# One core of Trainium2: block 1's first query, turned copy and scores moved behind the first query chunk, and new places for the first gathers

## The chip, the core and the metric

The kernel runs on one core of a Trainium2 chip. The metric is the device time of one launch in microseconds (us). The data are 32-bit floats throughout.

## The reference, cut to what matters

Two transformer-like blocks work one behind the other on 256 tokens of width 1024. The change lies in the last part of the second block: the end of the cross attention and the feed-forward stage with looked-up experts (PEER). For every token and each of 8 heads that stage picks 16 of 16384 experts by two small top-16 searches, and adds their outputs:

```python
def block(xb):                                   # 128 tokens, called for two blocks
    qh = (xb @ w_pq).reshape(T, P_HEADS, 2, P_KEY_DIM)
    s1 = einsum('thd,nd->thn', qh[:, :, 0], sub_keys1)
    s2 = einsum('thd,nd->thn', qh[:, :, 1], sub_keys2)
    v1, i1 = top_k(s1, 16);  v2, i2 = top_k(s2, 16)
    cand_s = v1[..., :, None] + v2[..., None, :]
    top_s, pos = top_k(cand_s.reshape(T, 8, 256), 16)
    eidx = the 16 expert numbers of pos
    g = softmax(top_s)
    a = gelu(einsum('thkd,td->thk', expert_down[eidx], xb))
    return einsum('thk,thkd->td', g * a, expert_up[eidx])
h = h + peer_ffn(rmsnorm_2(h, g_ffn), ...)
return rmsnorm_2(h, g_final)
```

## The kernel before, in words

**Layout.** One program per engine, tied by semaphores that only count up. Each engine takes its instructions in the order in which they are written down, so a wait holds up all that stands behind it on that engine.

**Groups, rows, steps.** The PEER stage has 16 groups g = 0 to 15: g // 8 is the block of 128 tokens (t), g % 8 the head (h). A group has 16 rows; row i of group g is called row g.i here. A row is one indirect DMA, which fetches for each of the 128 tokens one expert's down and up vector, 8 KB, so 1.05 MB in all (`gathers_pool`, L2058; the DMA is L2079). For each group the vector engine works in four steps q of four rows (`STEPS0` for group 0, `STEPS` for the others). A step is: the four dot products with the token (`down_dve`, L2083), a part of the search for a later group (`route_dve`), then, after ScalarE's gelu of the four results (`gelu`, L1954), the coefficients (`coef_dve`) and the weighted sums of the up vectors (`up_dve`, L2123). From group 1 on, some rows are "turned": ScalarE makes a diagonal matrix of the coefficients and TensorE adds the row (`weigh`, L1872). The indices of group 1 are searched for whole behind step 1 of group 0. Step 0's gelu of group 1, like those of steps 0 to 3 of group 0, stands among ScalarE's query work, at places written out by hand.

**Places.** A row is fetched into one of 16 places of 2048 floats per partition (`GPAIR`, L1125). Many of them are memory that earlier work still uses. `SOON` names those that are free early; group 0 uses only these, in turn, so its later rows wait until an earlier row's sum is made. `late` gives the memory of the others, `LATEWAIT` (L2054) what the Pool queue waits for before it uses one for the first time: the end of a query chunk (`s_chunk`), which frees a ring buffer, or the scores of a head (`s_ps`). Place 13 is ring buffer 2 and waits for the end of the last query chunk, before and after the change.

**Queries.** Head 0 has a query of its own, made per token block from the weights PQ0 (`query0_pe`, L1611), so that group 0 can start early: block 0's while block 1's projection is still to come. Heads 1 to 7 take one weight chunk each, called c1 to c7 here (`queries(h)`, L1866): 16 matmuls over all 256 tokens. TensorE writes a chunk into two of the four banks of psD, and ScalarE evicts it (`pair_act`, L1158). Three matmuls into chunk c(h), TensorE makes the scores of head h - 1 (`scores`, L1857), for which c(h-1) must have been evicted; ScalarE scales those (`scored`, L1907). The weights of c1 to c4 and c7 lie in the ring (c7's are loaded by the SP queue when c3 has ended, L2252), those of c5 and c6 in PQ5 and PQ6, fetched by the Pool queue. `xturn_pe` (L1626) turns block 1's state back to tokens along partitions, `xturn_act` scales it into XTOK, the other operand of the dot products.

**Order around the change.** TensorE (`blocks_pe`, L1635): block 0's projection and turn, query, scores and turned copy; block 1's cross output, residual and projection; the turn of block 1's state; block 1's query for head 0 (L1667, L1668), its turned copy (L1669) and its scores (L1670, L1671); then c1 to c7. ScalarE has the matching evictions at the end of `blocks_act` (L1800 to L1804), then in `peer_act` eight diagonals and, for each h, what L1918 to L1931 say. The Pool queue loads PQ5 (L2333), for which it waits until block 1's residual is in, and goes on to the gathers. Rows 0.4 to 0.8 wait each until the row four before it has landed (L2075).

Of the kernel before, what the change touches and what calls it, by code (L numbers as in the profile page):

```python
# [59 lines left out]
SLOT = {i: k for k, i in enumerate(i for _, turned in STEPS for i in turned)}  # L60
NT = len(SLOT)
SLOT.update({12: SLOT[5], 14: SLOT[6]})
SOON = [4, 5, 6, 9, 10, 11, 12, 0, 3]

MQK_SCALE = MQK ** -0.5
MAGIC = 1.5 * 2.0 ** 23
# [98 lines left out]
def build(nc, a):  # L165
# [875 lines left out]
    def ff2_act(dst, T):  # L1041
        for mg in range(4):
# [77 lines left out]

    slot = lambda v: v.rearrange("p k t -> p (k t)")[:, 0:2 * D]
    soon = [carve([2 * D]) for _ in range(6)] + [VT[:, 0:2].rearrange("p a d -> p (a d)"), slot(ZS), slot(SQ)]
    late = {1: slot(feat[:, 3]), 2: slot(ring[:, 3]), 7: slot(ring[:, 0]), 8: slot(ring[:, 1]), 13: slot(ring[:, 2]),
            14: slot(XN), 15: slot(feat[:, 4])}
    GPAIR = [soon[SOON.index(i)] if i in SOON else late[i] for i in range(PTOP)]  # L1125
    XP = soon[3].rearrange("p (n h s) -> p n h s", n=4, h=2)
# [409 lines left out]
    XTURN = {(0, 0): psD[:, 2], (1, 0): psD[:, 3], (0, 1): psD[:, 2], (1, 1): psD[:, 3]}  # L1536
    XSUM = {(0, 0): psD[:, 0], (0, 1): psD[:, 1], (1, 0): psD[:, 2], (1, 1): psD[:, 3]}
    HTURN = {(0, 0): psD[:, 2], (0, 1): psB[:, 0], (1, 0): psD[:, 0], (1, 1): psD[:, 1]}
    QBANK = {(0, 0): psB[:, 1], (0, 1): psD[:, 0], (1, 0): psB[:, 0], (1, 1): psB[:, 1]}
    SBANK = {(0, 0): psD[:, 1], (0, 1): psD[:, 2], (1, 0): psD[:, 2], (1, 1): psD[:, 3]}  # L1540
    s_xw = sem("s_xw")
    s_acc, s_ht, s_xh, s_rs, s_h3 = (sem(n) for n in ("s_acc", "s_ht", "s_xh", "s_rs", "s_h3"))

# [67 lines left out]
    def query0_pe(t, m):  # L1611
        if t:
            nc.tensor.wait_ge(s_ttc, m + 1)
        for k in range(KT):
            if m == 0 and k % 4 == 0:
                nc.tensor.wait_ge(s_xh, 2 * t + k // 4 + 1)
            mm = nc.tensor.matmul(QBANK[t, m][:, 0:P], PQ0[:, k, m * P:(m + 1) * P], XN2[:, k, blk(t)], start=(k == 0),
                                  stop=(k == KT - 1))
        mm.then_inc(s_qh, 1)

    def score0_pe(t, x):
        nc.tensor.wait_ge(s_qe, 2 * t + x + 1)
        (nc.tensor.matmul(SBANK[t, x][:, 0:PK], QH[:, x, blk(t)] if t else QH0[:, x], SKT[:, x], start=True, stop=True)
         .then_inc(s_ps, 1))
# [10 lines left out]
    def blocks_pe():  # L1635
        for j in range(4):
            chunk_pe(FIRST["xq"], j, XN2, T2, fresh=5 if j == 0 else None)
            if j:
                cross_scores_pe(j - 1)
        cross_scores_pe(3)  # L1640
        cross_turn_pe(0, 0)
        cross_turn_pe(1, 0)
        residual_pe(0)
        cross_out_pe(0, 0)
        cross_turn_pe(0, 1)
        project_pe(0, (0, 1), range(4))
# [12 lines left out]
        xturn_pe(0)
        cross_out_pe(1, 0)  # L1660
        cross_out_pe(1, 1)
        residual_pe(1)
        project_pe(1, (0, 1), range(8))
        project_pe(1, (2, 3), range(8))
        hturn_pe(1, 0)
        hturn_pe(1, 1)
        query0_pe(1, 0)  # L1667
        query0_pe(1, 1)  # L1668
        xturn_pe(1)  # L1669
        score0_pe(1, 0)  # L1670
        score0_pe(1, 1)  # L1671

    XSCALE = float(XD) ** -0.5

# [75 lines left out]
        nc.scalar.activation(dst, QBANK[t, m][:, 0:P], ACT.Identity).then_inc(s_qe, 1)  # L1750

    def score0_act(t, x):
        nc.scalar.wait_ge(s_ps, 2 * t + x + 1)
        if x == 0:
            nc.scalar.wait_ge(s_rs, t + 1)
        dst = SCO[:, t, x] if t else SCO0[:, x]
        (nc.scalar.activation(dst, SBANK[t, x][:, 0:PK], ACT.Identity, scale=F7[:, t, 2:3])
         .then_inc(s_psc, 1))
# [9 lines left out]
    def blocks_act(first_gate, first_gelu):  # L1768
# [28 lines left out]
            ins.then_inc(s_xh, 1)  # L1797
        state_root_act(1)
        first_gelu()
        for m in range(2):  # L1800
            query0_act(1, m)
        xturn_act(1)
        for x in range(2):
            score0_act(1, x)  # L1804

    (s_sk, s_ps, s_psc, s_tt, s_ttc, s_eid, s_io, s_gel, s_coef, s_usev, s_uset, s_diag, s_fin, s_fsq, s_frt) = (
        sem(n) for n in (
# [42 lines left out]
    def peer_pe():  # L1850
# [4 lines left out]
        HOME.update({FIRST["pq"] + 4: (PQ5, s_mem, 32), FIRST["pq"] + 5: (PQ6, s_sk, 64)})  # L1855

        def scores(h):  # L1857
            nc.tensor.wait_ge(s_psc, max(h + 2, 4))
            nc.tensor.wait_ge(s_dev, FIRST["xq"] + 4 + h)
            for t in range(2):  # L1860
                for x in range(2):
                    mm = nc.tensor.matmul(psB[:, h % 2, (2 * t + x) * PK:(2 * t + x + 1) * PK],
                                          QH[:, 2 * h + x, t * P:(t + 1) * P], SKT[:, x], start=True, stop=True)
            mm.then_inc(s_ps, 1)

        def queries(h):  # L1866
            if h == 2:
                nc.tensor.wait_ge(s_psc, 4)
            chunk_pe(FIRST["pq"], h - 1, XN2, T2, clear=FIRST["xq"] + 2 + h,
                     mid=(lambda: scores(h - 1)) if h > 1 else None, place=3)  # L1870

        def weigh(t, g, fixed=1, first=False):  # L1872

# [31 lines left out]

    def peer_act(link):
        def scored(h):  # L1907
            nc.scalar.wait_ge(s_ps, h + 4)
            for t in range(2):
                ins = nc.scalar.activation(SCO[:, t, 2 * h:2 * h + 2],  # L1910
                                           psB[:, h % 2, t * T2:(t + 1) * T2].rearrange("p (x n) -> p x n", x=2),
                                           ACT.Identity, scale=F7[:, t, 2:3])
            ins.then_inc(s_psc, 2 if h == PH - 1 else 1)
# [2 lines left out]
            ins = nc.scalar.activation(DIAG[:, k], ident[:, :], ACT.Identity, scale=col("g_final_2", k))  # L1916
        ins.then_inc(s_io, 1)
        for h in range(1, PH):  # L1918
            if h == 6:
                coefficients(0, 3)  # L1920
            if h > 1:
                scored(h - 1)
            if h == 4:
                coefficients(0, 2)
            if h == 6:
                gate(1)
            if h == 7:
                gelu(1, 0)
            pair_act(FIRST["pq"], h - 1, QH[:, 2 * h:2 * h + 2])
            if h == 1:  # L1930
                coefficients(0, 1)  # L1931
        scored(PH - 1)
        nc.scalar.wait_ge(s_xs, 6)
        for g in range(1, 2 * PH):
# [79 lines left out]
    def route_dve(g, part, link, t=0, first=False):  # L2014
# [5 lines left out]
        if part == 0:  # L2020
            for r in ((0, 1), (1, 2)) if first else ((0, 2),):
                r = slice(*r)
                if t == 0:
                    nc.vector.wait_ge(s_psc, r.stop if first else g + 4)
                if not first:
                    link(nc.vector.tensor_scalar(SCOH, SCO.rearrange("p t x n -> p (t x) n")[:, bass.ds(2 * g, 2)], 1.0,
                                                 None, ALU.mult))
# [12 lines left out]
        if part == 3:  # L2040
            oh = OH.rearrange("p c k j -> p (c k) j")
            wide = [P, 2 * PTOP, PTOP]
            if first:
# [7 lines left out]
                                            in1=SELK[:, 1], op0=ALU.mult, op1=ALU.add).then_inc(s_eid, 1))  # L2051


    LATEWAIT = {1: (s_ps, 7), 2: (s_chunk, FIRST["pq"] + 4), 7: (s_chunk, FIRST["pq"] + 1),  # L2054
                8: (s_chunk, FIRST["pq"] + 2), 13: (s_chunk, FIRST["pq"] + 7), 14: (s_ps, PH + 3), 15: (s_ps, PH + 3)}


    def gathers_pool():  # L2058

        last = {}  # L2060
        for g in range(2 * PH):
            nc.gpsimd.wait_ge(s_eid, g + 1)
            for i in range(PTOP):
                b = pair(g, i)
                if b in last:
                    nc.gpsimd.wait_ge(*used(*last[b]))
                elif b == 3:
                    nc.gpsimd.wait_ge(s_qh, 4)
                elif g == 0 and i in (6, 7):
                    nc.gpsimd.wait_ge(s_h3, 4)  # L2070
                elif g == 0 and i == 0:
                    nc.gpsimd.wait_ge(s_xo, 4)
                elif b in LATEWAIT:
                    nc.gpsimd.wait_ge(*LATEWAIT[b])
                if g == 0 and 4 <= i < len(SOON):  # L2075
# [58 lines left out]
    def peer_dve(link, looped):  # L2134
# [47 lines left out]
        for g in range(2 * PH):  # L2182
# [4 lines left out]
            for q in range(len(steps(g))):  # L2187
                if g % PH == 0 and q == 0:
                    dve.wait_ge(s_ttc, 2 * (g // PH) + 2)
                down_dve(g, q, g)  # L2190
                if g == q == 0:
                    rstd_dve(1)
                for h, part in routes(g, q):
                    route_dve(h, part, link, h // PH)
# [62 lines left out]
    def _(pool):  # L2257
# [71 lines left out]
        g.iota(IOI, pattern=[[1, PTOP]], base=0, channel_multiplier=0).then_inc(s_io, 1)  # L2329
        pool.wait_ge(s_io, 1)  # L2330
        g.tensor_copy(IOTA, IOI).then_inc(s_io, 1)
        pool.wait_ge(s_xs, 5)
        pool.dma_start(PQ5.rearrange("p k n -> p (k n)"), a["pq5"]).then_inc(s_mem, 16)  # L2333
        gathers_pool()

    @block.scalar
# [268 lines left out]
```

## Time and profile before

| | us |
|---|---|
| median of three timed runs | 1513.57 (1513.55 to 1515.67) |
| the profiled execution's own time | 1514.97 |
| its span, first to last instruction | 1513.2 |

| engine | busy, share of the span |
|---|---|
| PE (TensorE matmul) | 84% |
| DVE (vector engine) | 64% |
| POOL | 34% |
| ACT (ScalarE) | 23% |

The profiled execution is 1.4 us above the median, and its span leaves out 1.8 us around the first and the last instruction. Times of rows are counted from the span's start. The mean granted clock of TensorE over the span is 0.912 of its full speed. The PEER stage begins near 841 us with block 0's first query; its first gather is issued at 855 us. From about 870 us to 1500 us the row of the page that gives the DMA engines' share in 40 slices stands at 9 tenths or more in every slice.

How to read it: a timeline row gives start, duration, engine, line, operation and operands, and in brackets the idle time of the engine just before it with what ended it. A DMA's row on POOL is only its issue. The DMA view gives for a stretch each kind of transfer issued in it, with its median time from issue to landing. Matmuls are pipelined and their ends are modelled.

### The profile page before, as it was taken

How to read it: one execution, taken by the hardware profiler on the slowest of the kernel's cores; microseconds unless marked ns; L12 is line 12 of the kernel's file. 1: busy time of each engine (PE TensorE's matmuls, PEld its weight loads, DVE VectorE, ACT ScalarE, POOL GpSimd, SP SyncE). 2: the span in 40 equal slices, each digit the busy share in tenths (PEclk: the TensorE clock that was granted, in tenths of full speed). 3: DMA queues.
4: the chain of work that ended last, by engine and by line, in shares of the span. 5: the costliest groups of instructions: out<-in, count | busy, mean ns of one | idle time of the engine just before them, and what ended most of it. 6: DMA issues, size and time to landing. Idle time of an engine off the chain costs nothing.

```text
span 1513.2 us, 14840 instructions
## 1 busy us (share of the span) xinstructions
PE 1266.0 (84%) x5254; PEld 907.0 (60%) x5254; DVE 970.1 (64%) x1897; ACT 350.0 (23%) x718; POOL 510.4 (34%) x407
## 2 busy tenths in 40 slices
PE   8999999999999999999999998665755666556656
PEld 6776778888888888887888896222222222222222
DVE  7799985153410000324422499999999998999987
ACT  3443433222100000123412332111111211111112
POOL 3367771010000000000010256666545555555550
PEclk9999999999999999999999999888687777887788
DMA  6232333253344444333264499999999999999997
GB/s 265 84 112 84 112 115 137 88 195 139 139 158 148 156 150 151 135 133 112 84 241 180 166 405 414 421 421 421 422 422 422 421 423 422 422 421 422 422 421 298
DMA packets 55018, 389.60 MB, mean 257 GB/s; under 512 B 6192, under 2 KB 6512, under 8 KB 8240
## 3 DMA queue, kind: packets, MB, share of 16 engines
q0 software_dynamic: 38400, 278.15, 44.4%
q1 hardware_dynamic: 16416, 110.64, 20.6%
q8 instruction: 37, 0.61, 0.1%
q14 instruction: 21, 0.17, 0.0%
q10 hardware_dynamic: 144, 0.03, 0.0%
HBM read 387.75 MB, written 1.05 MB: 257 GB/s over the span
## 4 chain that ended last, share of the span: by engine, by line
PE 52%; DVE 21%; DMA 18%; POOL 4%; issue 3%; ACT 2%; DVEq 0%; ACTq 0%; POOLq 0%
PE psD L992 12%; DMA arena<-in_expert,arena 9%; PE psD L935 8%; PE psD L1036 7%; PE psD L416 7%; DMA ring<-in_expert,arena 5%; DMA feat<-in_expert,arena 4%; PE psD L1009 4%; DVE arena L2090 3%; DVE feat L2090 2%; POOL arena L2079 2%; PE psD L1595 2%; DVE ring L2090 2%; PE psD L1366 2%; DVE feat L2123 2%
## 5 line engine op out<-in xcount | busy, mean ns | idle before, releaser
L992 PE MATMUL psD<-feat,ring 128*128 128x256 f32 (+1 forms) x1056 | 234.0, 382 | 5.7 <-DVE feat L370 5.2
L992 PEld LDWEIGHTS psD<-feat,ring 128*128 128x128 f32 x1056 | 201.4, 191 | 34.8 <-issue 6.5
L2079 POOL DMA_INDIRECT feat<-in_expert,arena x77 | 107.9, 1401 | 178.8 <-DVE arena L2050 156.9
L2324 POOL DMA_DIRECT2D feat<-in_xo x3 | 1.7, 554 | 443.4 <-PE psN L345 443.4
L2079 POOL DMA_INDIRECT arena<-in_expert,arena x102 | 132.2, 1296 | 38.1 <-issue 26.8
L2090 DVE CUSTOM_DVE_ANT_0 arena<-arena,feat 128x1024 f32<-128x1024 f32 x102 | 121.5, 1222 | 24.2 <-DMA arena<-in_expert,arena 23.9
L935 PE MATMUL psD<-feat,ring 128*128 128x256 f32 (+1 forms) x576 | 133.5, 390 | 0.0
L1884 PE MATMUL psB<-arena 128*128 128x512 f32 x128 | 82.8, 805 | 50.9 <-ACT arena L1977 50.9
L935 PEld LDWEIGHTS psD<-feat,ring 128*128 128x128 f32 x576 | 108.7, 191 | 24.7 <-issue 8.1
L416 PE MATMUL psD<-feat,ring 128*128 128x256 f32 x512 | 110.8, 379 | 0.0
L1036 PE MATMUL psD<-feat,ring 128*128 128x256 f32 x512 | 110.7, 379 | 0.0
L416 PEld LDWEIGHTS psD<-feat,ring 128*128 128x128 f32 x512 | 97.3, 190 | 13.2
L1036 PEld LDWEIGHTS psD<-feat,ring 128*128 128x128 f32 x512 | 97.3, 190 | 13.2
L2079 POOL DMA_INDIRECT ring<-in_expert,arena x60 | 87.1, 1451 | 31.7 <-issue 14.3
L2090 DVE CUSTOM_DVE_ANT_0 feat<-feat 128x1024 f32<-128x1024 f32 x77 | 92.2, 1221 | 7.7 <-DMA feat<-in_expert,arena 7.1
L1884 PE MATMUL psB<-feat,arena 128*128 128x512 f32 x96 | 68.1, 868 | 32.7 <-ACT arena L1977 32.7
L1960 ACT ACTIVATE arena<-arena 128x4 f32<-128x4 f32 (+2 forms) x68 | 14.1, 207 | 347.5 <-DVE arena L2090 347.5
L1884 PEld LDWEIGHTS psB<-arena 128*128 128x128 f32 x128 | 31.6, 259 | 102.1 <-ACT arena L1977 64.9
L331 DVE TENSOR_TENSOR feat<-feat 128x512 f32<-128x512 f32 x13 | 9.0, 690 | 121.4 <-ACT feat L304 121.3
L1884 PE MATMUL psY<-arena 128*128 128x512 f32 x56 | 40.7, 819 | 46.2 <-ACT arena L1977 46.2
L2090 DVE CUSTOM_DVE_ANT_0 ring<-ring,feat 128x1024 f32<-128x1024 f32 x60 | 73.1, 1219 | 8.5 <-DMA ring<-in_expert,arena 8.5
L1977 ACT ACTIVATE arena<-ident,arena 128x128 f32<-128x128 f32 x136 | 46.8, 395 | 126.5 <-DVE arena L2101 125.5
(559 smaller groups left out, 2201.8 us busy)
## 6 DMA issues: line engine op xcount, KB each, us to landing
ring<-in_w SPq DMA_DIRECT2D x101, 1024.0 KB, 4.8
feat<-in_xo POOLq DMA_DIRECT2D x3, 1024.0 KB, 8.4
feat<-in_pq POOLq DMA_DIRECT2D x2, 1024.0 KB, 11.5
arena<-in_expert,arena POOLq DMA_INDIRECT x102, 22.5
feat<-in_expert,arena POOLq DMA_INDIRECT x77, 19.5
feat<-in_xT SPq DMA_DIRECT2D x2, 544.0 KB, 4.5
arena<-in_w_akv POOLq DMA_DIRECT2D x1, 1024.0 KB, 5.3
feat<-in_memT POOLq DMA_DIRECT2D x1, 1024.0 KB, 5.8
```

Of the source, the lines that this page charges most:

```text
L416: mm = nc.tensor.matmul(psD[:, b + m, 0:T], ring[:, slot, k, m * P:(m + 1) * P], x[:, k], start=(k == 0), stop=(k == KT - 1))
L935: mm = nc.tensor.matmul(psD[:, m, 0:x.shape[2]], ring[:, slot, k, m * P:(m + 1) * P], x[:, k], start=(k == 0), stop=(k == KT - 1))
L992: mm = nc.tensor.matmul(psD[:, 2 * (c % 2) + m, 0:T], home[:, k, m * P:(m + 1) * P], x[:, k], start=(k == 0), stop=(k == KT - 1))
L1009: mm = nc.tensor.matmul(psD[:, 2 * (c % 2) + m, 0:T2], ring[:, c % RING, k, m * P:(m + 1) * P], YSB[:, k], start=(k == 0), stop=(k == KT - 1))
L1036: mm = nc.tensor.matmul(psD[:, 2 * (mg % 2) + m, 0:T], ring[:, c % RING, k, m * P:(m + 1) * P], x[:, KT * kg + k], start=(kg == 0 and k == 0),
L1366: mm = nc.tensor.matmul(vbank(h), x[:, k, g * P:(g + 1) * P], ring[:, c % RING, k, :], start=(k == 0), stop=(k == KT - 1), skip_group_chec ...
L1595: mm = nc.tensor.matmul(XSUM[t, j // 2][:, (j % 2) * CW:(j % 2) * CW + CW], OX[:, k, blk(t)], XOW[j][:, k, :], start=False, stop=True, ski ...
L1884: mm = nc.tensor.matmul(sums[t][half][:, 0:512], DIAG[:, SLOT[i]], row, start=first, stop=True, skip_group_check=True)
L1977: nc.scalar.activation(DIAG[:, k], ident[:, :], ACT.Identity, scale=COEF[:, i:i + 1]).then_inc(s_diag, 1)
L2079: (nc.gpsimd.indirect_dma_start(GPAIR[b], None, a["expert"], bass.IndirectOffsetOnAxis(ap=EID[:, c:c + 1], axis=0)) .then_inc(s_gb[b], 16))
L2090: (nc.vector.tensor_tensor_reduce(row, row, XTOK[:, like // PH], 1.0, 0.0, ALU.mult, ALU.add, AD[:, i:i + 1]) .then_inc(s_usev, 1))
L2123: ins = nc.vector.scalar_tensor_tensor(out=acc, in0=row, scalar=COEF[:, i:i + 1], in1=acc, op0=ALU.mult, op1=ALU.add)
```

## The change

TensorE starts c1 right behind the turn of block 1's state. Behind c1 come the turned copy, the scores of head 1, and block 1's first query; the first query's two scores stand inside c2, where the scores of head 1 stood. The banks change to match. ScalarE's list by h becomes another: the gelus of group 0's steps 2 and 3 stand ahead of the evictions of c3 and c4 (before: behind the scores of head 3, ahead of c4's; and ahead of the scores of head 5), group 1's exponential ahead of c5's, its step 0 gelu ahead of c6's (before: c7's). PQ5 is loaded behind row 0.5, not ahead of row 0.0. Group 0 has eight places instead of nine, each used twice, and the first uses of several places by group 1 wait for something else. The vector engine takes block 1's reciprocal root behind step 1's dots of group 0, not step 0's.

```diff
-SOON = [4, 5, 6, 9, 10, 11, 12, 0, 3]
+SOON = [4, 5, 6, 7, 9, 10, 11, 12]
...
-    late = {1: slot(feat[:, 3]), 2: slot(ring[:, 3]), 7: slot(ring[:, 0]), 8: slot(ring[:, 1]), 13: slot(ring[:, 2]),
+    late = {0: slot(ring[:, 0]), 1: soon[8], 2: slot(ring[:, 1]), 3: slot(feat[:, 3]), 8: slot(ring[:, 3]), 13: slot(ring[:, 2]),
             14: slot(XN), 15: slot(feat[:, 4])}
...
-    QBANK = {(0, 0): psB[:, 1], (0, 1): psD[:, 0], (1, 0): psB[:, 0], (1, 1): psB[:, 1]}
-    SBANK = {(0, 0): psD[:, 1], (0, 1): psD[:, 2], (1, 0): psD[:, 2], (1, 1): psD[:, 3]}
+    QBANK = {(0, 0): psB[:, 1], (0, 1): psD[:, 0], (1, 0): psB[:, 0], (1, 1): psD[:, 3]}
+    SBANK = {(0, 0): psD[:, 1], (0, 1): psD[:, 2], (1, 0): psB[:, 0], (1, 1): psY[:, :]}
...
         hturn_pe(1, 1)
-        query0_pe(1, 0)
-        query0_pe(1, 1)
-        xturn_pe(1)
-        score0_pe(1, 0)
-        score0_pe(1, 1)
...
         first_gelu()
-        for m in range(2):
-            query0_act(1, m)
-        xturn_act(1)
-        for x in range(2):
-            score0_act(1, x)
...
         def scores(h):
-            nc.tensor.wait_ge(s_psc, max(h + 2, 4))
+            nc.tensor.wait_ge(s_psc, max(h + 2, 5) if h > 1 else 2)
+            if h == 1:
+                nc.tensor.wait_ge(s_ttc, 2)
...
         def queries(h):
-            if h == 2:
-                nc.tensor.wait_ge(s_psc, 4)
-            chunk_pe(FIRST["pq"], h - 1, XN2, T2, clear=FIRST["xq"] + 2 + h,
-                     mid=(lambda: scores(h - 1)) if h > 1 else None, place=3)
+            chunk_pe(FIRST["pq"], h - 1, XN2, T2, clear=FIRST["xq"] + 2 + h, ready=entered if h == 1 else None,
+                     mid=None if h == 1 else later_scores if h == 2 else lambda: scores(h - 1), place=3)
+            if h == 1:
+                xturn_pe(1)
+                scores(1)
+                query0_pe(1, 0)
+                query0_pe(1, 1)
+
+        def entered(k):
+            if k % 4 == 0:
+                nc.tensor.wait_ge(s_xh, 3 + k // 4)
+
+        def later_scores():
+            nc.tensor.wait_ge(s_ttc, 3)
+            score0_pe(1, 0)
+            score0_pe(1, 1)
...
         for h in range(1, PH):
+            if h > 2:
+                scored(h - 1)
+            if h in (3, 4):
+                coefficients(0, h - 1)
+            if h == 5:
+                gate(1)
             if h == 6:
-                coefficients(0, 3)
-            if h > 1:
-                scored(h - 1)
-            if h == 4:
-                coefficients(0, 2)
-            if h == 6:
-                gate(1)
-            if h == 7:
                 gelu(1, 0)
             pair_act(FIRST["pq"], h - 1, QH[:, 2 * h:2 * h + 2])
             if h == 1:
                 coefficients(0, 1)
+                scored(1)
+                xturn_act(1)
+                query0_act(1, 0)
+                query0_act(1, 1)
+                score0_act(1, 0)
+                score0_act(1, 1)
...
-    LATEWAIT = {1: (s_ps, 7), 2: (s_chunk, FIRST["pq"] + 4), 7: (s_chunk, FIRST["pq"] + 1),
-                8: (s_chunk, FIRST["pq"] + 2), 13: (s_chunk, FIRST["pq"] + 7), 14: (s_ps, PH + 3), 15: (s_ps, PH + 3)}
+    LATEWAIT = {0: (s_chunk, FIRST["pq"] + 1), 1: (s_qh, 4), 2: (s_chunk, FIRST["pq"] + 2), 3: (s_ps, 7),
+                8: (s_chunk, FIRST["pq"] + 4), 13: (s_chunk, FIRST["pq"] + 7), 14: (s_ps, PH + 3), 15: (s_ps, PH + 3)}
...
-                elif b == 3:
-                    nc.gpsimd.wait_ge(s_qh, 4)
+                elif g == 0 and i == 3:
+                    nc.gpsimd.wait_ge(s_xt, 4)
+                elif g == 0 and i == 4:
+                    nc.gpsimd.wait_ge(s_xo, 4)
                 elif g == 0 and i in (6, 7):
+                    if i == 6:
+                        nc.gpsimd.wait_ge(s_xs, 5)
+                        nc.gpsimd.dma_start(PQ5.rearrange("p k n -> p (k n)"), a["pq5"]).then_inc(s_mem, 16)
                     nc.gpsimd.wait_ge(s_h3, 4)
-                elif g == 0 and i == 0:
-                    nc.gpsimd.wait_ge(s_xo, 4)
...
-                if g == q == 0:
+                if g == 0 and q == 1:
                     rstd_dve(1)
...
-        pool.wait_ge(s_xs, 5)
-        pool.dma_start(PQ5.rearrange("p k n -> p (k n)"), a["pq5"]).then_inc(s_mem, 16)
         gathers_pool()
```

Left out are the counts of the waits on `s_psc`, `s_ps` and `s_rs` that follow from the new order (the vector engine's search for group 1 waits for the scores of head 1, as before).

## Rows read from the trace of the kernel before

**Rows 1.** Windows: length, busy PE, PEld, DVE, ACT, POOL, clock, DMA share, GB/s

```profile
904.00:916.00 12.00, 12.00 (x65) 10.79 (x64) 11.86 (x21) 4.07 (x9) 9.16 (x7) 1.00 0.91 350
880.00:904.00 24.00, 24.00 (x125) 21.44 (x124) 22.97 (x69) 5.20 (x12) 9.39 (x8) 1.00 1.01 419
916.00:1500.00 584.00, 364.83 (x614) 148.13 (x613) 539.15 (x1146) 107.01 (x263) 319.22 (x231) 0.79 1.01 421
```

**Rows 2.** Timeline of the Pool queue, 850 to 940 us

```profile
852.41 0.56 POOL L2333 DMA_DIRECT2D feat<-in_pq  x1 [66.56 <-PE psD L1583]
855.24 1.03 POOL L2079 DMA_INDIRECT arena<-in_expert,arena  x1 [2.27 <-DVE arena L2050]
...
869.94 1.31 POOL L2079 DMA_INDIRECT feat<-in_expert,arena  x1 [1.19 <-DMA arena<-in_expert,arena]
...
903.52 1.92 POOL L2079 DMA_INDIRECT ring<-in_expert,arena  x1 [3.84 <-PE psD L992]
...
908.24 1.96 POOL L2079 DMA_INDIRECT arena<-in_expert,arena  x1 [0.30 <-DVE VT L2123]
...
926.92 1.69 POOL L2079 DMA_INDIRECT ring<-in_expert,arena  x1 [2.94 <-PE psD L992]
...
936.35 1.97 POOL L2079 DMA_INDIRECT feat<-in_expert,arena  x1 [4.21 <-DVE arena L2050]
```

**Rows 3.** DMA view, stretches at 852, 855, 870, 903.5, 908, 927, 936: us to landing

```profile
feat<-in_pq POOLq DMA_DIRECT2D x1, 1024.0 KB, 5.0
...
arena<-in_expert,arena POOLq DMA_INDIRECT x1, 5.5
...
feat<-in_expert,arena POOLq DMA_INDIRECT x1, 9.5
...
ring<-in_expert,arena POOLq DMA_INDIRECT x1, 6.4
...
arena<-in_expert,arena POOLq DMA_INDIRECT x1, 10.9
...
ring<-in_expert,arena POOLq DMA_INDIRECT x1, 12.1
...
feat<-in_expert,arena POOLq DMA_INDIRECT x1, 10.2
```

**Rows 4.** Timeline of TensorE, 867 to 929 us

```profile
867.73 3.89 PE L1617 MATMUL psB<-feat 128*128 128x128 f32 x32 [0.46 <-ACT feat L1795]
...
872.78 8.37 PE L992 MATMUL psD<-feat,ring 128*128 128x256 f32 x38
...
928.39 1.95 PE L1893 MATMUL psD<-arena,ones 128*128 128x128 f32 x16
```

**Rows 5.** Timeline of ScalarE: evictions of chunks (L1161), gelus (L1960), scores, turned copy

```profile
872.09 0.69 ACT L1765 ACTIVATE feat<-psY,arena 128x512 f32<-128x512 f32 x1 [0.16 <-PE psY L1631]
...
879.89 0.60 ACT L1161 ACTIVATE feat<-psD 128x512 f32<-128x512 f32 x1 [3.69 <-PE psD L992]
881.16 0.21 ACT L1960 ACTIVATE arena<-arena 128x4 f32<-128x4 f32 x1 [0.68 <-DVE arena L2090]
882.07 0.84 ACT L1910 ACTIVATE feat<-psB,arena 128x256 f32<-128x256 f32 x2 [0.71 <-PE psB L1862]
...
900.05 0.21 ACT L1960 ACTIVATE arena<-arena 128x4 f32<-128x4 f32 x1 [1.54 <-DVE arena L2090]
...
912.86 0.21 ACT L1960 ACTIVATE arena<-arena 128x4 f32<-128x4 f32 x1 [1.18 <-DVE arena L2090]
...
926.69 0.60 ACT L1161 ACTIVATE feat<-psD 128x512 f32<-128x512 f32 x1 [2.13 <-PE psD L992]
```

**Rows 6.** Timeline of the vector engine: the dot on row 0.7

```profile
879.90 1.22 DVE L2090 CUSTOM_DVE_ANT_0 feat<-feat 128x1024 f32<-128x1024 f32 x1
```

**Rows 7.** Windows of the kernel's start, where TensorE stood idle for 5 us

```profile
10.00:15.00 5.00, 0.02 (x1) 0.00 (x0) 4.76 (x15) 1.77 (x2) 0.00 (x0) 0.73 1.01 412
15.00:19.00 4.00, 3.82 (x9) 2.92 (x10) 3.93 (x14) 0.00 (x0) 0.00 (x0) 0.50 1.02 415
```

More of the change, by code:

```diff
@@ L1614, in query0_pe @@
         for k in range(KT):
-            if m == 0 and k % 4 == 0:
-                nc.tensor.wait_ge(s_xh, 2 * t + k // 4 + 1)
+            if t == m == 0 and k % 4 == 0:
+                nc.tensor.wait_ge(s_xh, k // 4 + 1)
             mm = nc.tensor.matmul(QBANK[t, m][:, 0:P], PQ0[:, k, m * P:(m + 1) * P], XN2[:, k, blk(t)], start=(k == 0),
@@ L1752, in score0_act @@
     def score0_act(t, x):
-        nc.scalar.wait_ge(s_ps, 2 * t + x + 1)
+        nc.scalar.wait_ge(s_ps, 3 * t + x + 1)
         if x == 0:
@@ L1907, in scored @@
         def scored(h):
-            nc.scalar.wait_ge(s_ps, h + 4)
+            nc.scalar.wait_ge(s_ps, h + 4 if h > 1 else 3)
+            if h == 1:
+                nc.scalar.wait_ge(s_rs, 2)
             for t in range(2):
@@ L2023, in route_dve @@
                 if t == 0:
-                    nc.vector.wait_ge(s_psc, r.stop if first else g + 4)
+                    nc.vector.wait_ge(s_psc, r.stop if first else 3 if isinstance(g, int) and g == 1 else g + 4)
                 if not first:
```

## The prediction

> **What bounds the kernel now.** I read the windows first. From 880 to 1500 us the 16 DMA engines are busy for a share of 1.01 and move 419 to 421 GB/s, with one dip: 350 GB/s from 904 to 916 [rows 1]. So the last 650 us are set by bytes: 256 gathers of 1.05 MB, each 1.05/421 = 2.49 us of the engines. The vector engine is 92% busy in 916 to 1500 and still keeps up. What can move the end is the moment at which the stream starts, and every stretch in which no gather is issued. The POOL timeline shows the dip's cause: row 1.2 went out at 903.52 after 3.84 us of waiting for a query chunk [rows 2]. It cost 12 x (1 - 350/421) = 2.0 us. The time from issue to landing tells how far ahead the queue is: 6.4 us for row 1.2, which found the engines dry, 12.1 us for row 1.13 issued at 926.92 [rows 3]. So before the change row 1.13 may be 5.7 us later before the stream breaks again. It waits for chunk c7's weights to leave their ring buffer. The question is when c7 ends.
>
> **Pool queue, start.** The load of PQ5 is taken away ahead of row 0.0. It was issued at 852.41 and landed after 5.0 us at 857.4, in time in which the engines had nothing else; row 0.0 could not be issued before 855.24, when its index was ready, and landed 5.5 us later [rows 2, 3]. That is 4.5 us behind its own 1.03 us of issue, as with row 1.2 (6.4 less 1.92), so row 0.0 gains next to nothing. Behind row 0.5 the same 1.05 MB costs its full 2.49 us of a running stream, unless it fills a hole. The hole it may fill: row 0.6 now waits for block 1's projection, which ends two turns ahead of the first query at 867.73 [rows 4], near 866; rows 0.0 to 0.5 keep the engines in work until past 870, so there is none. Bounds: 0 and 2.5 us; I take **+2.0**. Row 0.7 landed at 869.94 + 9.5 = 879.4 [rows 2, 3], now at 881.4.
>
> **Places.** Eight instead of nine: row 0.8 waits for row 0.0's add, which ended near 873.5, so it goes out about 1 us later. Rows 0.5 to 0.7 and PQ5 are then still under way: nothing. Rows 0.12 to 0.15 wait for adds that end up to 888, with row 0.11 landing only near 891: nothing. In head 1, row 1.2 now needs c2 (ring buffer 1) and row 1.3 the scores of head 3, both there by 903.5; the dip of 2.0 us goes: **-2.0**. The first twelve rows of head 1 stand, by this, where they stood. The SP queue's last load (c7's weights) waits for c3; 4 us later it still has 20 us to spare.
>
> **TensorE and ScalarE, chunk by chunk.** A chunk is 32 matmul instructions; 38 run in 872.78 to 880.98, so 0.216 us each, 6.9 us a chunk, and with 0.9 us of scores 7.8 a head; evictions of c1 at 879.89 and c7 at 926.69 say the same, 46.8/6 [rows 4, 5].
> - c1 starts at 867.73, where the first query started, and ends at 874.7: 5.0 us **earlier**. The moved work follows it: turned copy 0.9, scores of head 1 from 875.6 to 876.5, first query 3.6, to 880.1. (Its 32 instructions ran from 867.73 to 871.46; turned copy and the two small scores filled the 1.3 us from there to c1 [rows 4], 0.9 and 0.4.) Six instructions of c2 end at 881.4. Up to here nothing is lost or won.
> - There TensorE waits for ScalarE, which has put step 1's gelu of group 0 first. That gelu waits for the vector engine's dot on row 0.7: it ran at 881.16 [rows 5]. With the row at 881.4 the dot (879.90 before, 1.22 long [rows 6]) ends at 882.7, 1.6 us later. Then gelu 0.2, scores 0.84, the turned copy's halves 1.3 together, and 0.55 for the first query's two evictions [rows 5]: 885.7. TensorE goes on at 886.0 after the two small scores; 26 instructions: c2 ends at 891.6, which was 887.5. **+4.1.**
> - c3 ends at 899.4. Its eviction now stands behind step 2's gelu of group 0, which waits for vector work: 900.05 before [rows 5], 901.65 with the 1.6. Evicted at 902.5; scores of head 3 start at 902.6 and not 900.7: **+1.9**. c4 ends at 909.1.
> - c4's eviction stands behind step 3's gelu, two heads sooner than before. That gelu ran at 912.86 [rows 5]; it can't be earlier, because the vector engine is busy for 34.8 of the 36 us from 880 to 916 [rows 1] and gets no work taken off. At 914.5 now; c4 evicted at 915.3, scores of head 4 at 915.4 instead of 910.4: **+5.0**. c5 ends at 921.9.
> - c6 at 929.7, c7 at **937.5** instead of 926.5: 11.0 us late. (Step 0's gelu of group 1, ready near 926, stands ahead of c6's eviction at 929.9 and costs nothing.)
>
> **Clock.** After 5 us of idle TensorE, 10 to 15 us, the granted clock was 0.50, its lower level of 1.2 GHz, in 15 to 19 us; the four us of work at half speed cost 2.0 [rows 7]. The two new waits are 4.6 and 5.0 us long. What the first costs is swallowed by the second, which ends when the gelu ends. The second may add 0 to 3 us; I take **+1.5**. The Trainium skill (TensorE: Matmul & The Clock Gate, HAM oscillation) says that each such wait can start the next matmuls cold; by it the term would be near 2, by a trace in which only long idles show it, perhaps 0.
>
> **The sum.** Row 1.13 goes out 10.8 us late, at 937.7. Issued at a dry stream it lands 6.4 us later, 944.1, and not at 926.92 + 12.1 = 939.0: **+5.1**. This contains the 2.0 and the -2.0 above. A stream that starts again isn't full at once: row 1.2 landed at 909.9, row 1.5 at 908.24 + 10.9 = 919.1 [rows 2, 3], 9.2 us for three transfers of 2.49, **+1.7**. With the clock: 5.1 + 1.7 + 1.5 = **+8.3**. From there nothing gives it back: the stream is full in every later window, and the end hangs on the last landing. The profiled execution took 1515.0 us (span 1513.2), 1.4 over the median of 1513.6. So 1523.3 on its terms, **1521.9** on the median's.
>
> Unknown ends: if row 0.7 is not late (-1.6), the lone gather lands in 5.5 us (-0.9), the stream restarts at once (-1.7) and the clock holds (-1.5), +2.6 is left, 1516.2. With 3 us of clock and 2.5 for the vector engine's lateness instead of 1.6, +10.7, 1524.3.
>
> **The vector engine.** ScalarE must see 16 matmuls of TensorE (928.39 [rows 4]) before it goes on to group 1's step 1, whose product the vector engine wanted as soon as group 2's index was made, at 936.3 [rows 2]. With c7 at 937.5 and the last scores and those matmuls behind it, gelu 1.1 comes near 942.3: the vector engine stands some 5 us, 6.5 with the clock. It then lags by 6.5 to 8 us, the gathers by 8, so it isn't the bound: a head takes it 92% of the stream's 39.8 us.
>
> **Rivals.** What a measurement of this kernel tells from no change is 0.2%, 3 us.
> - **Row 1.13 is in time, not slower (0.13).** It decides at c7's end: up to 932.2 (5.7 us late) the queue doesn't run dry. That needs c4's eviction not to wait for step 3's gelu, 5 us less. Then what is left is +2.0 for PQ5 and -2.0 for the dip, 1513.6; should PQ5 find a hole after all, 1511.6. For it: the first twelve rows do get out sooner. Against it: in the code the gelu stands ahead of the eviction, and the vector engine has no gap to be earlier in. The Trainium skill (Perfetto Trace Analysis, Identifying the Most-Contended Engine) has it that the most contended engine sets the time. Here that would be the DMA engines with the same bytes, and no change, 1513.6; the dip in [rows 1] speaks against reading it so.
> - **The vector engine becomes the bound (0.07).** If its stand near 937 is over 10 us, places come free too late in head 2 and a second hole opens, some 5 us: 1527. The 10.2 us from issue to landing of row 2.0 [rows 2, 3], 3.8 more than at a dry queue, and the 8 us by which the stream itself is late speak against it.
> - **Only part of it (0.10).** c7 late by 7 to 9 us, 1515 to 1517.
> - **My forecast (0.70)**, 1517 to 1525.
>
> Range 1515 to 1526: it leaves out the first rival and most of the second. Faster 0.05 (half of PQ5 hidden, row 1.13 in time), same 0.11, slower 0.84.
>
> **What would show it.** Right: PQ5 issued near 865; row 1.2 issued before 902; TensorE waiting 4 to 5 us in the scores inside c2 and again inside c5, behind ScalarE; c7's eviction near 938; row 1.13 issued then and landing within 7 us; a window of 936 to 944 well under 420 GB/s and none after it. Wrong: row 1.13 landing 10 us or more after its issue, or DMA at 1.01 throughout.

## The result and the profile after

The changed kernel takes 1523.45 us (median of 5 runs, 1522.87 to 1525.43), the kernel of before 1514.88 (5 runs, 1513.55 to 1515.67): a ratio of 1.0060 with a 95% interval of 1.0049 to 1.0071, so 8.6 us slower. Forecast were +8.3 us and 1521.9.

The profiled execution of the changed kernel has this first line:

```profile
span 1522.2 us, 14829 instructions
```

Its own time is 1523.96 us. From 60 us up to the change TensorE's instructions start 1.0 us later than in the profile of before, long ahead of anything that the change touches: the residual's first matmul (L1583) starts at 820.34 instead of 819.30. "Corrected" below means less this 1.04. From that matmul to the last instruction it is 701.9 us, and was 693.9. This stretch I call the stage; it is 8.0 longer.

The windows of the changed kernel, columns as in [rows 1]:

```profile
880.00:904.00 24.00, 19.48 (x93) 16.91 (x92) 21.23 (x56) 5.33 (x14) 9.82 (x8) 0.86 1.01 408
904.00:916.00 12.00, 8.60 (x44) 7.35 (x42) 11.83 (x27) 0.98 (x3) 7.96 (x6) 0.98 1.01 425
916.00:936.00 20.00, 19.02 (x87) 16.88 (x88) 17.65 (x36) 6.65 (x13) 7.59 (x5) 0.84 1.01 420
936.00:946.00 10.00, 8.89 (x54) 7.70 (x52) 4.97 (x11) 2.57 (x6) 2.48 (x3) 1.00 0.30 102
946.00:1500.00 554.00, 337.80 (x518) 130.96 (x519) 512.09 (x1097) 100.44 (x249) 306.98 (x225) 0.77 1.01 421
```

The dip of [rows 1] from 904 to 916 is gone (425 GB/s). A hole has come instead: 102 GB/s from 936 to 946, 10 x (1 - 102/421) = 7.6 us of the stream. After it the stream is full to the end.

The Pool queue's timeline has the reason:

```profile
856.28 1.04 POOL L2092 DMA_INDIRECT arena<-in_expert,arena  x1 [69.38 <-DVE arena L2060]
...
867.49 0.59 POOL L2084 DMA_DIRECT2D feat<-in_pq  x1
...
871.16 1.30 POOL L2092 DMA_INDIRECT feat<-in_expert,arena  x1 [1.14 <-DMA arena<-in_expert,arena]
...
903.32 1.06 POOL L2092 DMA_INDIRECT ring<-in_expert,arena  x1 [0.30 <-issue]
...
925.28 1.99 POOL L2092 DMA_INDIRECT feat<-in_expert,arena  x1 [0.30 <-issue]
942.25 0.94 POOL L2092 DMA_INDIRECT ring<-in_expert,arena  x1 [14.97 <-PE psD L992]
944.15 0.94 POOL L2092 DMA_INDIRECT feat<-in_expert,arena  x1 [0.97 <-PE psB L1854]
```

Row 1.2 goes out at 903.32 without a wait. Row 1.12 goes out at 925.28, and then the queue waits 14.97 us for TensorE's last query chunk: row 1.13 goes out at 942.25, corrected 941.2, and not at 926.92 [rows 2].

ScalarE's timeline, evictions of chunks in L1161, gelus in L1970:

```profile
875.96 0.60 ACT L1161 ACTIVATE feat<-psD 128x512 f32<-128x512 f32 x1 [1.07 <-PE psD L992]
884.48 0.21 ACT L1970 ACTIVATE arena<-arena 128x4 f32<-128x4 f32 x1 [7.93 <-DVE arena L2103]
...
895.75 0.60 ACT L1161 ACTIVATE feat<-psD 128x512 f32<-128x512 f32 x1 [6.92 <-PE psD L992]
...
903.38 0.21 ACT L1970 ACTIVATE arena<-arena 128x4 f32<-128x4 f32 x1 [4.61 <-DVE arena L2103]
903.55 0.60 ACT L1161 ACTIVATE feat<-psD 128x512 f32<-128x512 f32 x1
...
916.15 0.21 ACT L1970 ACTIVATE arena<-arena 128x4 f32<-128x4 f32 x1 [9.58 <-DVE arena L2103]
916.26 0.58 ACT L1161 ACTIVATE feat<-psD 128x512 f32<-128x512 f32 x1
...
926.41 0.60 ACT L1161 ACTIVATE feat<-psD 128x512 f32<-128x512 f32 x1 [4.88 <-PE psD L992]
...
942.01 0.60 ACT L1161 ACTIVATE feat<-psD 128x512 f32<-128x512 f32 x1 [4.77 <-PE psD L992]
```

The evictions of c2, c3, c4, c5 and c7 stand at 895.75, 903.55, 916.26, 926.41 and 942.01. c4's follows 0.1 us behind the gelu of step 3 of group 0, which waited 9.58 us for the vector engine. TensorE's timeline shows what that does to the chunks:

```profile
881.24 1.46 PE L992 MATMUL psD<-feat,ring 128*128 128x256 f32 x6
887.22 0.77 PE L1623 MATMUL psB<-arena,feat 128*128 128x128 f32 x2 [4.52 <-ACT feat L1745]
...
888.21 8.79 PE L992 MATMUL psD<-feat,ring 128*128 128x256 f32 x32
...
911.14 1.46 PE L992 MATMUL psD<-feat 128*128 128x256 f32 x6
916.98 2.05 PE L1854 MATMUL psB<-arena,feat 128*128 128x128 f32 x8 [4.38 <-ACT feat L1161]
918.82 7.55 PE L992 MATMUL psD<-feat 128*128 128x256 f32 x26
```

Two new waits: 4.52 us inside c2, 4.38 us inside c5. Each is followed by slow matmuls. The windows give the granted clock (third column from the right, ahead of the DMA engines' share and the GB/s):

```profile
883.00:885.00 2.00, 0.00 (x0) 0.00 (x0) 1.55 (x5) 0.29 (x2) 0.00 (x0) 0.96 1.00 414
885.00:891.00 6.00, 3.78 (x11) 3.27 (x12) 5.93 (x11) 2.98 (x8) 3.73 (x3) 0.50 1.02 422
892.00:912.00 20.00, 20.00 (x102) 17.82 (x101) 19.38 (x55) 3.04 (x7) 8.91 (x8) 1.00 1.00 407
917.00:922.00 5.00, 5.00 (x16) 4.37 (x17) 4.90 (x10) 2.43 (x5) 2.02 (x3) 0.50 1.01 421
923.00:941.00 18.00, 18.00 (x93) 16.06 (x92) 15.58 (x32) 4.37 (x8) 3.96 (x2) 1.00 0.78 325
```

From 885 to 891 and from 917 to 922 us it is 0.50, the level of 1.2 GHz; between and after, 1.00. The 26 matmul instructions after the second wait took 7.55 us, where 5.78 is the rule at full clock, and the eight of the scores 2.05 instead of 1.05.

### The profile page after: what moved, and what is told of

Its sections match the earlier page's. It is cut to its first block, busy times and chain, and to the rows that moved or that the text cites. A ratio compares the mean times of both kernels' runs of the same rounds, so it can differ in the third digit from the quotient of the medians.

```text
span 1522.2 us, 14829 instructions
## 1 busy us (share of the span) xinstructions
PE 1265.5 (83%) x5254; PEld 908.6 (60%) x5254; DVE 970.2 (64%) x1897; ACT 349.9 (23%) x718; POOL 504.8 (33%) x407
## 3 DMA queue, kind: packets, MB, share of 16 engines
HBM read 387.75 MB, written 1.05 MB: 255 GB/s over the span
## 4 chain that ended last, share of the span: by engine, by line
PE 52%; DVE 22%; DMA 17%; issue 3%; POOL 3%; ACT 1%; DVEq 0%; ACTq 0%; POOLq 0%
PE psD L992 13%; PE psD L935 8%; DMA arena<-in_expert,arena 7%; PE psD L416 7%; PE psD L1036 7%; DMA VT<-in_expert,arena 5%; DMA feat<-in_expert,arena 5%; PE psD L1009 4%; DVE arena L2103 3%; DVE feat L2103 2%; PE psB L1888 2%; POOL arena L2092 2%; PE psD L1366 2%; DVE ring L2103 2%; DVE feat L2136 1%
## 5 line engine op out<-in xcount | busy, mean ns | idle before, releaser
L2092 POOL DMA_INDIRECT arena<-in_expert,arena x102 | 136.4, 1338 | 116.8 <-DVE arena L2060 69.4
L1970 ACT ACTIVATE arena<-arena 128x4 f32<-128x4 f32 (+2 forms) x68 | 14.1, 207 | 359.9 <-DVE arena L2103 359.9
L1888 PE MATMUL psB<-feat,arena 128*128 128x512 f32 x100 | 72.0, 877 | 29.5 <-ACT arena L1987 29.5
```

The lines of the kernel that those rows point to most:

```text
L1888: mm = nc.tensor.matmul(sums[t][half][:, 0:512], DIAG[:, SLOT[i]], row, start=first, stop=True, skip_group_check=True)
L1970: nc.scalar.activation(v, v, ACT.Gelu).then_inc(s_gel, 1)
L2092: (nc.gpsimd.indirect_dma_start(GPAIR[b], None, a["expert"], bass.IndirectOffsetOnAxis(ap=EID[:, c:c + 1], axis=0)) .then_inc(s_gb[b], 16))
```

## The experiments

Each kernel changes the changed kernel, or the one of before, at one place or a few. Since single executions differ ahead of the change (more on this at the end), each profile is also read by its stage: from the start of the residual's first matmul to the last instruction. The table has all of them. "Row 1.13" is its issue, counted from that same matmul. The ratio is to before's runs of the same series (medians 1514.88 down to a_pq5_first, 1514.14 from b_gelu3_sooner to a_order_back_pq5_first, 1514.36 for the two repeats). The last column is explained behind the table.

| kernel | median us, runs | ratio to before, 95% | stage us | row 1.13 | stage less row 1.13 | stage less the stream's loss |
|---|---|---|---|---|---|---|
| before | 1514.88, 5 | | 693.9 | 107.6 | | 691.8 |
| before_again | 1514.45, 11 | 0.9990 to 1.0008 | 693.3 | 107.6 | | 691.7 |
| the changed kernel | 1523.45, 5 | 1.0049 to 1.0071 | 701.9 | 121.9 | 580.0 | 690.8 |
| a_gelu3_later | 1518.19, 9 | 1.0012 to 1.0032 | 695.4 | 115.1 | 580.3 | 690.8 |
| a_first_evictions | 1522.32, 4 | 1.0038 to 1.0071 | 699.5 | 119.4 | 580.1 | 691.7 |
| a_order_back | 1517.03, 10 | 1.0005 to 1.0024 | 693.8 | 107.7 | | 691.1 |
| a_pq5_first | 1521.16, 4 | 1.0027 to 1.0060 | 698.6 | 118.5 | 580.1 | 691.5 |
| b_gelu3_sooner | 1523.06, 4 | 1.0045 to 1.0076 | 699.9 | 118.6 | 581.3 | 691.0 |
| b_pq5_behind | 1516.12, 10 | 1.0003 to 1.0022 | 695.1 | 108.4 | | 691.6 |
| a_busy_wait | 1521.81, 4 | 1.0037 to 1.0067 | 699.3 | 119.3 | 580.0 | 691.3 |
| a_order_back_pq5_first | 1514.57, 11 | 0.9994 to 1.0012 | 692.0 | 107.7 | | 690.6 |
| the same again | 1514.23, 11 | 0.9990 to 1.0008 | 692.0 | 107.7 | | 690.8 |

"Stage less row 1.13" is the finding in one line. Where row 1.13 goes out at 115.1 or later, the stage ends 580.0 to 581.3 us after its issue, whatever made it late. Where it is at 108.4 or sooner, its time no longer matters. The border lies between; by the margin of 5.7 us in the prediction it would be near 113.3, and no run falls there.

The last column checks this by the stream. Over the 75 us from 60 to 135 us behind the residual I take what the stream misses against 421 GB/s (0.2 to 8.9 us), and add the 2.49 us of PQ5 where it is loaded behind row 0.5. The stages differ by 9.9 us, from 692.0 to 701.9; less this loss, all twelve are 690.6 to 691.8. So the stage is longer by what the stream missed or moved in addition, to within 1.2 us.

One thing the runs don't part: in each of them row 1.13 is late because c7 ends late. No run gives this row alone another place with c7 still late. Rows 1.14 and 1.15 stand right behind it and wait for the scores that follow c7; in the changed kernel row 1.14 goes out 1.9 us after row 1.13.

**b_gelu3_sooner: one part alone, on the kernel of before.**

```diff
-            if h == 6:
-                coefficients(0, 3)
             if h > 1:
                 scored(h - 1)
             if h == 4:
                 coefficients(0, 2)
+                coefficients(0, 3)
```

> The kernel of before with one line moved: ScalarE's step 3 gelu of group 0 ahead of c4's eviction instead of two heads later. TensorE's order, places and PQ5 are as before. Late-gather theory: c4 is evicted at 913.1 instead of 903.3, TensorE stands for some 9 us, its clock falls, c7 is evicted near 939 instead of 926.7; row 1.13, which had 5.7 us to spare, lands near 945.5 instead of 939.0 and the stream has a hole as in the changed kernel: +7 to +9, 1522 to 1524. Rival, the hole needs the new order of TensorE or PQ5's place: under +3.

Measured: 1523.06, the whole loss of the change by one moved call. TensorE, the Pool queue and the DMA rate of this kernel:

```profile
914.58 2.04 PE L1862 MATMUL psB<-arena,feat 128*128 128x128 f32 x8 [9.15 <-ACT feat L1161]
916.42 6.49 PE L992 MATMUL psD<-feat 128*128 128x256 f32 x26
```

```profile
938.78 1.65 POOL L2078 DMA_INDIRECT ring<-in_expert,arena  x1 [13.91 <-PE psD L992]
```

```profile
936.00:942.00 6.00, 5.22 (x36) 4.62 (x34) 6.00 (x9) 1.44 (x3) 2.92 (x2) 1.00 0.20 41
```

TensorE stands for 9.15 us inside c5, row 1.13 waits 13.91 us, and the stream moves nearly nothing. Neither TensorE's new order nor PQ5's place is needed for the hole. This run also speaks on the vector engine as the bound. Its waits for ScalarE's gelus (engine, what waited, what for, total, times, longest):

```profile
DVE arena L2097 <- ACT arena L1959: 9.8, 2, 8.7
```

It stands 8.7 us at one place here, and 5.3 us in the changed kernel, whose stage is 2.0 us longer. So the time doesn't follow this wait. Row 1.13 is 3.3 us sooner than in the changed kernel and the stage only 2.0 shorter, since the dip of 904 to 916 is still there: here the stream misses 8.9 us in all, in the changed kernel 8.6 and PQ5's 2.49.

**a_gelu3_later: undo the last of ScalarE's three blocks.**

```diff
-            if h in (3, 4):
-                coefficients(0, h - 1)
+            if h == 3:
+                coefficients(0, 2)
             if h == 5:
+                coefficients(0, 3)
                 gate(1)
```

> The changed kernel, with ScalarE's step 3 gelu of group 0 one head later: behind the eviction of c4, ahead of c5's. Late-gather theory (row 1.13 goes out when c7 ends, the stream is dry until then): c4 is evicted at its natural time near 911 instead of 916.3, TensorE doesn't stand and its clock holds, so c7 is evicted near 935 instead of 942. Row 1.13 is due near 933, so 5 to 6 us of the hole go: 1517.5 to 1518.5. Rival, PQ5 behind row 0.5 sets the time: no change, 1523. Rival, the vector engine sets it through its 5.3 us wait for gelu 1.1 (946.5): that wait shrinks to about 0 and the time falls by some 5 us too, so this run alone doesn't part the two; the DMA rate in the hole does.

Measured: 1518.19, 5.3 less than the changed kernel. c4's eviction, and the issue of row 1.13:

```profile
909.92 0.60 ACT L1161 ACTIVATE feat<-psD 128x512 f32<-128x512 f32 x1 [4.77 <-PE psD L992]
```

```profile
934.42 1.03 POOL L2093 DMA_INDIRECT ring<-in_expert,arena  x1 [8.22 <-PE psD L992]
```

c4 is evicted at its natural time, row 1.13 goes out 6.8 us sooner counted from the residual, and the stage becomes 6.5 shorter. The vector engine's wait for gelu 1.1 shrinks too, from 5.3 to 0.4 us, as both readings had it. The stream is what parts them: it misses 2.1 us here and 8.6 in the changed kernel, a difference of 6.5.

**a_first_evictions: undo the block in c2 alone.**

```diff
             if h == 1:
-                coefficients(0, 1)
                 scored(1)
                 xturn_act(1)
                 query0_act(1, 0)
                 query0_act(1, 1)
                 score0_act(1, 0)
                 score0_act(1, 1)
+                coefficients(0, 1)
...
-                if g == 0 and q == 1:
+                if g == q == 0:
                     rstd_dve(1)
```

> The changed kernel, with ScalarE's head 1 scores, turned copy, first query evictions and scores ahead of step 1's gelu of group 0, and the vector engine's reciprocal root back behind step 0's dots, so that TensorE doesn't stand inside c2. Late-gather theory: c2 is evicted near 888.7 (7 us sooner), but c3's eviction still waits for gelu 0.2 near 903.2 and c4's for gelu 0.3 near 916, so c5 to c7 don't gain more than the clock's 2 to 3 us: 1521 to 1523.5. Rival, delays of TensorE simply add up (each us saved in c2 comes back at the end): 7 us less, 1516.5.

Measured: 1522.32, 1.1 less; the stage is 2.4 shorter. TensorE:

```profile
883.30 0.38 PE L1623 MATMUL psB<-arena,feat 128*128 128x128 f32 x2
...
905.11 2.04 PE L1854 MATMUL psB<-arena,feat 128*128 128x128 f32 x8 [6.50 <-ACT feat L1161]
...
917.88 1.13 PE L1854 MATMUL psB<-arena,feat 128*128 128x128 f32 x8 [2.74 <-ACT feat L1161]
918.85 5.78 PE L992 MATMUL psD<-feat 128*128 128x256 f32 x26
```

The wait in c2 is gone, and with it 7 us of c2's lateness; but it comes back as a wait of 6.50 us in c4 for c3's eviction behind gelu 0.2, and 2.74 us in c5. Delays ahead of a gelu that comes at its own time don't add up. What was won is the clock: the wait in c5 is now so short that its 26 instructions run in 5.78 us.

**a_busy_wait: the clock by itself.** Ten unneeded matmuls are added; nothing is left out.

```diff
+            if h == 4:
+                nc.tensor.wait_ge(s_ttc, 4)
+                for i in range(10):
+                    nc.tensor.matmul(psN[:, 0:T2], ident[:, :], XN2[:, 0], start=True, stop=True)
             nc.tensor.wait_ge(s_dev, FIRST["xq"] + 4 + h)
```

> The changed kernel with 10 unneeded matmuls (128x256, 4.3 us at the full clock) into a free bank just before TensorE waits for c4's eviction. They fill the wait near 913 to 917. Clock term: c5 runs at the full clock and c7 comes 2.5 to 2.8 us sooner, row 1.13 too, 1521. If the clock doesn't matter, or falls all the same: 1523.5, or later if the added work outlasts the wait.

Measured: 1521.81; the stage is 2.6 shorter.

```profile
912.91 4.48 PE L1854 MATMUL psN<-feat,ident 128*128 128x256 f32 x20
917.71 1.16 PE L1858 MATMUL psB<-arena,feat 128*128 128x128 f32 x8 [0.32 <-ACT feat L1161]
918.71 5.78 PE L992 MATMUL psD<-feat 128*128 128x256 f32 x26
```

The added 20 instructions fill the wait down to 0.32 us, and c5's scores and matmuls run at the full clock (1.16 and 5.78 us). So the low clock after the second wait costs 2.6 us of the change.

**a_pq5_first: undo PQ5's place alone.** The wait on s_xs and the load go back ahead of `gathers_pool`, as before the change.

> The changed kernel with PQ5's load back ahead of row 0.0, nothing else. Late-gather theory: row 0.7 lands 2.5 to 2.8 us sooner, the vector engine's gelus 0.1 and 0.3 come that much sooner, c7 and row 1.13 too: 2.5 us less, 1521. The hole stays: the DMA rate near 940 still falls under 200 GB/s. Rival, PQ5's place sets the time: all of it goes, 1514 to 1515.

Measured: 1521.16, the stage 3.3 shorter. The hole stays (240 GB/s from 936 to 948). PQ5's place is a part of the loss, through the vector engine, and not its cause. Of the 3.3 us, 2.3 are the gelu of step 3, which comes that much sooner counted from the residual; 1.1 are the clock, as c5's 26 instructions took 6.45 us instead of 7.55.

**b_pq5_behind: the same part alone, on the kernel of before.** The load stands behind row 0.5, as in the change.

> The kernel of before with PQ5 loaded behind row 0.5, nothing else. The load moves from idle engines into the running stream, +2.5 to +2.8 at row 0.7's landing. But the dip at 904 (2.0 us), where row 1.2 waits for c4's end, is then covered by rows that are themselves 2.5 us late, so at the end only +0.5 to +1 is left: 1515.5 to 1516. If the dip is not covered: +2.5, 1517.4.

Measured: 1516.12, interval 0.5 to 3.3 us slower; stage +1.2. The dip covers a part of it: from 904 to 916 the stream moves 387 GB/s, so of the dip's 2.0 us 1.0 is left. It covered less than expected. Against before's 1514.14 in the same series the median is 2.0 slower, between what was written down for a covered dip and for one that isn't.

**a_order_back: ScalarE's order as before.** `a_first_evictions`, and ScalarE's list by h as it was:

```diff
+            if h == 6:
+                coefficients(0, 3)
             if h > 2:
                 scored(h - 1)
-            if h in (3, 4):
-                coefficients(0, h - 1)
-            if h == 5:
+            if h == 4:
+                coefficients(0, 2)
+            if h == 6:
                 gate(1)
-            if h == 6:
+            if h == 7:
                 gelu(1, 0)
```

> Both together: ScalarE's list by h as before the change (gelu 0.2 ahead of c4's eviction, gelu 0.3 ahead of c6's, gelu 1.0 ahead of c7's), and the first evictions ahead of gelu 0.1. TensorE's order, the places and PQ5 stay as changed. Late-gather theory: c7 ends near 928, row 1.13 goes out then, in time; no hole near 940, and the dip at 904 is gone. What is left is PQ5 in the running stream (+2.5) less the dip (-2.0): 1515 to 1516, the same as before. Rival, TensorE's new order (c1 ahead of the first query) or the eight places cost the time: still 1520 or more.

Measured: 1517.03; stage 693.8, as before. Its Pool queue and windows:

```profile
926.39 0.94 POOL L2094 DMA_INDIRECT ring<-in_expert,arena  x1 [0.83 <-PE psD L992]
...
937.98 1.97 POOL L2094 DMA_INDIRECT ring<-in_expert,arena  x1 [5.39 <-DVE arena L2062]
```

```profile
900.00:918.00 18.00, 18.00 (x93) 16.06 (x92) 17.66 (x44) 4.77 (x11) 10.89 (x9) 1.00 1.01 420
918.00:936.00 18.00, 14.70 (x74) 11.11 (x72) 17.61 (x33) 5.27 (x11) 11.57 (x7) 1.00 1.01 421
936.00:948.00 12.00, 7.54 (x13) 3.06 (x14) 11.45 (x32) 1.89 (x6) 8.49 (x6) 0.86 1.01 414
```

Row 1.13 goes out as early as before, with TensorE's new order and the eight places in force. No hole, no dip: the dip's 2.0 us pay for PQ5's. By the times it is 0.8 to 3.6 us slower than before, by the stage not; the median came out 1 us over what was expected. The stage is that of one profile, whose own time of 1514.25 is the shortest of the ten. So this run shows that the hole is gone with TensorE's order as changed, and not that the rest of the change is free to within 2 us.

**a_order_back_pq5_first: the best of both.** The same with PQ5 first.

> a_order_back with PQ5's load back ahead of row 0.0: what is left of the change is TensorE's order, the eight places and the new waits. Late-gather theory: no hole near 940, no dip at 904, PQ5 in idle time: 2.0 us faster than before, 1513. If the dip moves elsewhere or the end isn't set by the stream: 1514.9.

Measured: stage 692.0, 1.3 to 1.9 less than the two profiles of before; median 1514.57, not less. So I ran it and the kernel of before once more.

> The version with ScalarE's order as before and PQ5 first, a second time. Its first profile had 692.0 us from the residual's first matmul (817.91) to the end, 1.9 less than before, while its median was 0.4 above before's. If the stage's gain is real and the earlier part only scatters: 692.0 again, and over all its executions a median 0 to 2 us under before's. If the edited kernel is slower ahead of the change: that matmul past 820 in most executions, and the median as before.

> The kernel of before, unchanged, a second time. In the profiles so far a matmul that no variant touches (the residual's first, L1583) starts between 817.9 and 821.1 us, 819.30 in the profile of before. If that is scatter of single executions: this profile puts it anywhere in that band, the rest from there to the end is 693.9 again within 0.3, and the times agree with before. If instead every edited kernel is a little slower ahead of the change: 819.3 again, and the stage 693.9.

Measured: 692.0 again, and 1514.23; before_again 693.3 and 1514.45. Its residual's first matmul:

```profile
820.38 1.84 PE L1583 MATMUL psD<-ident,feat 128*128 128x128 f32 x15
```

So the same kernel has it at 819.30 and at 820.38: that part scatters by execution. Over 22 executions of the edited version the median is 1514.3, against 1514.1, 1514.4 and 1514.5 for before in the same two series. The stage's gain of over 1 us repeats, a gain in time can't be shown. Whether the earlier part is slower in the edited kernel on average stays open; two profiles of each don't tell. No version here is shown to be faster than the kernel of before.

## Why the prediction was right

The mechanism held: ScalarE's order holds back c4's eviction, c7 ends late, row 1.13 is issued at a dry stream, and nothing gives it back. The sizes of three terms were off, and that the sum still came out within 0.3 us is partly luck. Of the signs that the prediction named, PQ5 was issued at 866.5 (near 865), row 1.2 at 902.3 (before 902, so just missed), c7 was evicted at 941.0 (near 938), and the stream moved 57 GB/s from 936 to 944; the DMA view gives no time to landing for row 1.13. By its own steps, in corrected times:

- **Pool queue, start: +2.0.** Too small. Row 0.7's dot, which waited for the row, started at 882.2; before the change the row had landed at 879.4. So it was up to 2.7 us late, about the whole 2.49 us of the load, the upper end of the bounds. The gelu of step 1 was 2.3 late, not 1.6. Where no hole follows, PQ5's place costs the stage 1.8 us (a_order_back 693.8, a_order_back_pq5_first 692.0). The vector engine's wait for row 0.7, and further down its wait for gelu 1.1:

```profile
883.22 1.23 DVE L2103 CUSTOM_DVE_ANT_0 feat<-feat 128x1024 f32<-128x1024 f32 x1 [1.25 <-DMA feat<-in_expert,arena]
...
946.53 0.17 DVE L2114 TENSOR_TENSOR arena<-arena 128x4 f32<-128x4 f32 x1 [5.31 <-ACT arena L1970]
```

- **Places, dip: -2.0.** Right: row 1.2 without a wait, 425 GB/s in 904 to 916; and in a_order_back it balances PQ5.
- **Wait in c2: +4.1.** The wait itself was right (forecast 881.4 to 886.0, measured 881.7 to 886.2), but c2's eviction was 7.0 late, for the clock fell after it. That this would be swallowed held: c4 was evicted from 915.2 on, forecast 914.7 to 915.3. By then c3's eviction no longer waited for its gelu; c3 was late by itself, and the +1.9 was part of the 7.0.
- **Wait in c5: +5.0.** 4.4 us, as more of it had been used up. TensorE went on with the scores of head 4 at 915.9, forecast 915.4, since the gelu of step 3 was 2.25 us late and not 1.6.
- **Clock: +1.5, 0 to 3.** Too small: 2.6 us by a_busy_wait, 2.8 by the rows of c5.
- **c7: 11.0 us late, 12.5 with the clock.** 14.3 (942.01 less 1.04 against 926.69). The 0.5 us at the scores of head 4 and the 1.3 us that the clock cost more than forecast are the difference.
- **The restart: +1.7.** Wrong. Row 1.13's 14.3 us less the prediction's own margin of 5.7 make 8.6, and the stage was 8.0 longer than before's (8.6 than before_again's): nothing was lost on top. In the changed kernel the stream moves 33 GB/s from 942 to 944, 279 from 944 to 946 and 414 from 946 to 948, so it is nearly full 4 us after row 1.13's issue. Behind row 1.2 of the kernel of before it took 10 us: 258 GB/s from 904 to 906, 356 from 910 to 912 and 397 from 912 to 914. One difference is the row's own issue, 1.92 us for row 1.2 and 0.94 for row 1.13; no run tries whether that is the reason.
- **The vector engine:** stands 5.31 us at gelu 1.1, forecast 5 to 6.5; not the bound.

So the sum came out right with two errors that happen to cancel: c7 1.8 us later than forecast, the restart 1.7 us cheaper. The first rival needed c7 by 932.2 and had no change, 1513.6. a_order_back brings c7 there: its stage is before's (693.8), while its median is 0.8 to 3.6 us above before's, so by both readings the hole accounts for most of the loss of 8.6. The clock fell to 0.50 behind both waits, and the second cost 2.6 to 2.8 us. The Trainium skill (TensorE: Matmul & The Clock Gate, HAM oscillation) describes such waits, after which the next matmuls start cold; the trace agrees. The 2 that the prediction gave for this rule was nearer than the 1.5 that it took.

## What to carry to other kernels

In a stage bound by transfers, read for each transfer how far ahead of a dry queue it is issued: the time to landing less that of one issued at a dry queue. In this kernel a delay up to that margin was free, and each us beyond it was paid in full. And where one engine serves two others in a fixed order, moving its wait for the one ahead of its work for the other ties the two together: here one moved call cost 8 us of 1514.

## What the runs showed that I had not expected

- Two waits of 4.4 to 4.5 us each brought the clock to 0.50 for 6 us or so, at 885 to 891 and 917 to 922 us. A wait of 2.74 us didn't (a_first_evictions). A longer one did not cost more. Over the full clock's 1.05 and 5.78 us, the eight scores and 26 instructions behind the wait took 2.8 us more after 4.38 us, 1.7 after 4.73 (a_pq5_first), 2.1 after 6.50 (a_first_evictions, in c4) and 1.7 after 9.15 (b_gelu3_sooner: 2.04 and 6.49 us).
- The residual's first matmul, with identical code ahead of it, starts anywhere from 817.9 to 821.1 us in 12 profiles. Nearly all of the spread is there early: the start of one and the same TensorE instruction differs by 1.7 us between the profiles at 46 us, by 2.9 at 60 us and by 3.2 at 150 us and from there to the residual. It hides a gain of 1 to 2 us in the times, while the stage of two profiles of one kernel repeats within 0.6 us.
